# A decoder trunk on one core: x loaded by column halves around the first weight quantum, and the first norm's transposes in four PSUM banks

## The reference

```python
def _rmsnorm(x, g):
    y = x * rsqrt(mean(x * x, axis=-1) + 1e-6)
    return y * g
...
proj = _rmsnorm(h, norm_mix_even) @ w_in     # h = x at first; columns q, k, v, u, v' of 512 each
qa, ka, va, ub, vb = split(proj)
ws = where(causal, sgu_w, 0)                 # 4 x 128 x 128, used by the gated MLP
```

## Time and profile before

| | |
|---|---|
| time, median of 3 | 1388.93 us (1388.77 to 1390.04) |
| span of the profiled execution | 1387.2 us |
| time less span | 1.7 us |
| TensorE busy | 1364.8 us, 98% |
| VectorE, ScalarE busy | 82%, 73% |
| DMA, mean over the span | 315 GB/s |

### The profile page before, as it was taken

One profiled execution on the slowest core, in us unless ns is written; L12 is line 12 of the kernel. 1 busy time (PEld: TensorE's weight loads), 2 busy tenths in 40 slices (PEclk: granted clock), 3 DMA queues, 4 the chain that ended last, 5 costly groups with the idle time before them and its releaser, 6 DMA issues.

```text
span 1387.2 us, 19322 instructions
## 1 busy us (share of the span) xinstructions
PE 1364.8 (98%) x6874; PEld 1140.0 (82%) x6874; DVE 1133.7 (82%) x1154; ACT 1006.9 (73%) x1185; POOL 86.8 (6%) x117
## 2 busy tenths in 40 slices
PE   8999999999999999999999999999999999999997
PEld 7779989988788888888888888888888888888885
DVE  5675655556569999999999999899999989999996
ACT  5664544456548778778877877887787788788775
POOL 1201000000028500000000000000000000000010
PEclk9999999999999999999999999999999999999999
DMA  9457754353479999999999999999999999999960
GB/s 327 168 201 281 292 183 153 127 191 133 165 274 380 392 393 389 392 374 361 386 380 372 359 394 372 364 385 372 371 366 390 370 366 388 373 367 374 386 258 33
DMA packets 180621, 436.96 MB, mean 315 GB/s; under 512 B 4070, under 2 KB 8332, under 8 KB 180572
## 3 DMA queue, kind: packets, MB, share of 16 engines
q1 hardware_dynamic: 176816, 422.74, 82.8%
q0 software_dynamic: 3680, 13.54, 2.7%
q10 hardware_dynamic: 76, 0.02, 0.0%
HBM read 423.18 MB, written 13.11 MB: 315 GB/s over the span
## 4 chain that ended last, share of the span: by engine, by line
PE 93%; DVE 3%; ACT 3%; issue 1%; DMA 0%; ACTq 0%; DVEq 0%
PE ps L1607 26%; PE ps L1608 26%; PE ps L1609 26%; PE ps L1862 3%; PE ps L1864 3%; PE ps L1863 3%; PE ps L2134 2%; DVE w_lo L1054 1%; ACT w_hi L655 1%; DVE xt_lo L1093 0%; PE ps L1634 0%; PE ps L2102 0%; ACT e L710 0%; PE ps L1623 0%; PE ps L1617 0%
## 5 line engine op out<-in xcount | busy, mean ns | idle before, releaser
L1483 DVE TENSOR_TENSOR w_lo<-ring_a,w_hi 128x1024 fp32r<-128x1024 f32 x384 | 460.3, 1224 | 41.7 <-ACT w_hi L931 32.1
L931 ACT ACTIVATE w_hi<-ring_a 128x1024 fp32r<-128x1024 f32 x384 | 399.5, 1059 | 67.2 <-PE ps L1609 67.2
L1483 DVE TENSOR_TENSOR w_lo<-ring_b,w_hi 128x1024 fp32r<-128x1024 f32 x288 | 345.6, 1224 | 27.4 <-ACT w_hi L931 24.5
L1607 PE MATMUL ps<-w_hi,xg_hi 128*128 128x512 f32 x896 | 356.4, 398 | 0.0
L1608 PE MATMUL ps<-w_lo,xg_hi 128*128 128x512 f32 x896 | 353.0, 394 | 0.0
L1609 PE MATMUL ps<-w_hi,xg_lo 128*128 128x512 f32 x896 | 351.6, 392 | 0.0
L931 ACT ACTIVATE w_hi<-ring_b 128x1024 fp32r<-128x1024 f32 x288 | 300.8, 1058 | 55.3 <-PE ps L1609 55.3
L1054 DVE TENSOR_TENSOR w_lo<-ring_a,w_hi 128x1024 fp32r<-128x1024 f32 (+2 forms) x119 | 141.7, 1198 | 115.4 <-ACT w_hi L655 115.3
L655 ACT ACTIVATE w_hi<-ring_a 128x1024 fp32r<-128x1024 f32 (+2 forms) x119 | 121.9, 1033 | 129.7 <-PE ps L1864 65.2
L1607 PEld LDWEIGHTS ps<-w_hi,xg_hi 128*128 128x128 f32 x896 | 168.4, 188 | 38.6 <-DVE w_lo L1483 1.9
L1609 PEld LDWEIGHTS ps<-w_hi,xg_lo 128*128 128x128 f32 x896 | 168.3, 188 | 38.0
(11 more groups left out here) (333 smaller groups left out, 1387.0 us busy)
## 6 DMA issues: line engine op xcount, KB each, us to landing
ring_a<-in_moe_wg SPq DMA_DIRECT2D x40, 2048.0 KB, 9.8
ring_a<-in_moe_wu SPq DMA_DIRECT2D x32, 2048.0 KB, 9.9
ring_b<-in_moe_wd SPq DMA_DIRECT2D x32, 2048.0 KB, 9.7
ring_b<-in_moe_wu SPq DMA_DIRECT2D x24, 2048.0 KB, 10.3
ring_a<-in_moe_wd SPq DMA_DIRECT2D x24, 2048.0 KB, 9.5
ring_b<-in_moe_wg SPq DMA_DIRECT2D x16, 2048.0 KB, 10.4
ring_a<-in_ffn_wg SPq DMA_DIRECT2D x5, 2048.0 KB, 8.7
ring_a<-in_ffn_wu SPq DMA_DIRECT2D x5, 2048.0 KB, 7.8
```

The costliest lines, as they stand in the source:

```text
L931: nc.scalar.activation(w_hi[:, (Q1 + q) % NQ, 0:1024], slot(j % RING2)[:, 1024 * k:1024 * k + 1024], ACT.Copy).then_inc(hi_done, 1)
L1483: v.tensor_tensor(w_lo[:, (Q1 + q) % NQ, 0:1024], slot(j % RING2)[:, 1024 * k:1024 * k + 1024], w_hi[:, (Q1 + q) % NQ, 0:1024].bitcast(F32 ...
L1607: pe.matmul(out_, a_hi, w_hi[:, q, c0:c1], start=first, stop=False)
```

## The change

x is loaded in two pieces by column halves (both row tiles in each, rows of 2 KB in place of 4 KB), and q's first quantum is issued between them; the second half has a semaphore of its own, `x_rest`. The four groups of the first norm go into banks 6, 7, 2 and 3, so that no group waits for a bank; the fillers are now 6 ahead of x's first half and 6 between the halves (before: 8, 4 and 3), in bank 4. ScalarE's sums of squares wait for both halves.

```diff
         def fbank(k):
+            if k < 4:
+                return (6, 7, 2, 3)[k]
             return k % 2 if fills["mix_odd"] <= k < fills["mix_odd"] + 4 else 6 + k % 2
...
             sp.dma_start(table[:, 0:P], consts_d[:, 0:P]).then_inc(ident_in, 16)
-            for t in range(T):
-                sp.dma_start(h[:, t, :], A["x"][0].rearrange("(t p) d -> p t d", p=P)[:, t]).then_inc(x_in, 16)
+            x_rows = A["x"][0].rearrange("(t p) d -> p t d", p=P)
+            sp.dma_start(h[:, :, 0:512], x_rows[:, :, 0:512]).then_inc(x_in, 16)
             lead = units[0]
             per = lead.shape[0] // lead.quanta
             for k in range(lead.quanta):
+                if k == 1:
+                    sp.dma_start(h[:, :, 512:D], x_rows[:, :, 512:D]).then_inc(x_rest, 16)
                 sp.dma_start(slot(0)[:, k * lead.quantum:(k + 1) * lead.quantum].rearrange("p (c n) -> p c n", c=per),
...
-            act.wait_ge(x_in, 16 * T)
+            act.wait_ge(x_in, 16)
+            act.wait_ge(x_rest, 16)
...
             def bank_free(k):
-                if k >= 2:
+                if k >= 4:
                     pe.wait_ge(*emptied(k - 2))
...
-            keep_pace(8, 3, P)
-            pe.wait_ge(x_in, 16 * T)
-            for f in range(4):
+            keep_pace(6, 4, P)
+            pe.wait_ge(x_in, 16)
+            for f in range(2):
                 turn("mix_even", f, h_chunk)
-                if f == 1:
-                    keep_pace(4, 3, P)
-                elif f == 2:
-                    keep_pace(3, 3, P)
+            keep_pace(6, 4, P)
+            pe.wait_ge(x_rest, 16)
+            for f in range(2, 4):
+                turn("mix_even", f, h_chunk)
```

More of the change, by code:

```diff
@@ L307, in slot @@
             return ring_a[:, s] if s < RING1 else ring_b[:, s - RING1]
-        ident_in, const_in, x_in, lead_gain_in, grow_in, gain_in, even_in, bands_in, odd_in, rw_in = map(sem, (
-            "ident_in", "const_in", "x_in", "lead_gain_in", "grow_in", "gain_in", "even_in", "bands_in", "odd_in", "rw_in"))
+        ident_in, const_in, x_in, x_rest, lead_gain_in, grow_in, gain_in, even_in, bands_in, odd_in, rw_in = map(sem, (
+            "ident_in", "const_in", "x_in", "x_rest", "lead_gain_in", "grow_in", "gain_in", "even_in", "bands_in", "odd_in", "rw_in"))
         loaded = [sem(f"loaded{s}") for s in range(RING2)]
```

## The result

| | before | after |
|---|---|---|
| median (19 executions each) | 1389.08 us | 1391.61 us |
| lowest to highest | 1388.56 to 1390.55 | 1390.03 to 1392.95 |
| ratio | | 1.0016, 95% interval 1.0009 to 1.0023 |
| span of the profiled execution | 1387.2 us | 1390.9 us (its time 1392.65) |

The change makes the kernel slower by 2.5 us, 0.16 to 0.18%. That is inside the 0.2% that I called no change, but the interval excludes 1, and 1391.61 is 1.4 us above the top of my range. The profiled execution is the third slowest of the 19, so its span (+3.7) shows more than the median (+2.5).

A forecast was written before the change was run, and what follows sets the result against it. TensorE, busy 98% at full clock, was taken as the bound. A 2.25 us earlier start was lost to k's weights (1.1) and the mask (1.05), rounding to 0: 1388.9 us, range 1387.7 to 1390.2.

The forecast's parts named there:

- Step 1: Load queue at the start: x's halves land at 5.3 and 8.0 us, q's last quantum still at 12.0.
- two bounds: Effect of 2 KB rows at the queue's start: landings from 0.84 us earlier to 1.3 us later; 0 was taken.
- Step 2: Fillers ahead of x: with 6 calls the transposes start at 5.6 instead of 6.65, 1.05 us earlier.
- Step 3: Four banks: no bank wait for the second transposes; q projection starts at 9.9 instead of 12.16, 2.25 us earlier.
- Step 4: k's weights: w_lo is ready near 22.6 as before, so TensorE stands 1.1 us and keeps 1.15 us.
- Step 5: Masked sgu_w: the mask still ends at 26.4, TensorE stands 1.05 us, and none of the gain is kept.
- I find nothing later than 26.6 that differs: After sgu_w's transposes: the rest of the kernel keeps its times, leaving the span at 1387.2 us.
- The earlier mask: At sgu_w: the mask comes earlier, saving up to k's 1.15 us, 1387.8 us at best; chance 0.15.
- the fully kept 2.25 us: At the start: k's weights and the mask both over a microsecond earlier, time 1386.7 us; chance 0.03.
- The row limit: At the queue's start: x's first half lands up to 1.3 us later, time 1389.3 to 1390.2; chance 0.16.
- The falling clock: In TensorE's new pauses at 21.5 and 25.5 us: clock falls to 1.2 GHz, 1391.7 us or more; chance 0.03.

The follow-up runs named there:

- Experiment 1: The changed kernel with one wait less on ScalarE: only x_rest is waited for, issued behind the first half; 1389.11 us, ratio 0.9999.
- Experiment 5: The changed kernel with one wait less on ScalarE, and sgu_w's transposes behind k's second quantum instead of its first; 1388.61 us, ratio 0.9993.
- Experiment 8: The kernel before with the first norm's four groups in four banks and the fillers in bank 4, x still loaded by rows; 1389.12 us, ratio 0.9998.
- Experiment 2: The kernel before with nothing but one redundant wait on ScalarE, for a semaphore long set; 1392.32 us, ratio 1.0020.
- e7: The changed kernel with ScalarE's square root table load moved behind all but the last of the y_rows_out copies; 1390.00 us, ratio 1.0007.
- e6: The kernel before with two redundant waits on ScalarE, packed into one instruction (a shift of 1); 1392.49 us, ratio 1.0022.
- e10: The kernel before with 64 redundant waits on ScalarE, a shift of 32 instructions; 1391.43 us, ratio 1.0014.
- e9: The kernel before with 16 redundant waits on ScalarE, a shift of 8 instructions; 1391.91 us, ratio 1.0016.
- e5: The changed kernel with five filler products of 128x256 in TensorE's wait ahead of the last item's scatter; 1390.88 us, ratio 1.0014.

## Why the prediction was wrong, by its own steps

- **Step 1, x by halves: right but for 0.45 us.** q's last piece landed at 12.5 where I had 12.0, and k's at 20.9 where I had 20.3. The term is small beside what it varies by: GpSimd's first issue, which waits for q's last piece, stands between 12.23 and 13.39 us in the seven profiled executions with x's halves (mean 12.63), and between 11.98 and 12.74 in the seven with x by rows (mean 12.31). A loss of 0.3 us by the shorter rows is in line with that and not shown by it; my two bounds (-0.84, +1.3) hold it. That both kinds of rows are alike once under way I read from three of the page's four rows of such loads: the fourth, `ring_b<-in_moe_wg` with 2 KB rows, has 10.4 us.
- **Steps 2 and 3: right.** Transposes at 5.72 (5.6 forecast), the second set without a bank's wait, the first q product at 9.98 (9.9). The reason that I gave for the banks costing nothing was wrong in part: VectorE empties the fourth group only at 14.8, after q has begun. It costs nothing because q is written to banks 0 and 1, and k's products, which need banks 2 and 3, begin at 23.28.
- **Step 4, k's weights: right in kind.** TensorE stood 1.48 us (1.1 forecast), since the landing was 0.6 later; 0.53 us was kept in place of 1.15. Experiment 1, where k's `w_hi` began at 20.19, kept 1.25.
- **Step 5, the mask: right in kind, the number by luck.** The transposes of `sgu_w` start at 26.55, inside the forecast 26.5 to 26.7. The last landing was 0.5 earlier than I had, and the mask took 1.21 us instead of 0.68, which happened to make up for it. In experiment 1 the mask took 0.71 us, the transposes start at 25.97, and 0.65 us was kept where I had 0. Experiments 5 and 8 agree with the mask as the wait that decides.
- **The step that failed** is the sentence behind it, "I find nothing later than 26.6 that differs". The sum has no term for the added wait on ScalarE: I put it at nothing without giving a reason. For its own time that is right, for its place in the program it is not. Experiments 1 and 2 show that this one instruction is the whole loss of 2.5 us, some 1357 us later, at a loop that the change doesn't touch: there TensorE stands 2.41 us ahead of the scatter instead of 0.87. The pause of 0.91 us at that loop's exit was in the trace of before; I hadn't looked at the tail, since nothing of the change was there. None of the rivals had this either.
- **The rivals.** The earlier mask and the fully kept 2.25 us didn't come. The row limit could have given up to 1390.2, and the landings don't show it: x's first half landed at 4.9, ahead of the forecast 5.3. The falling clock's time, 1391.7, lies beside the measured 1391.61 by chance: most of the loss is the late scatter, the clock costs 1.6 us where it falls instead of 2.8, and it falls behind the tail's pause. At the place that I named it was seen in one profiled execution (`e7`), at a pause of 1.91 us; I had put a pause of 1.1 there, and the spread of k's landing, which I had no row for, makes it longer at times.

How the 2.5 us divide: the scatter's start is 1.44 us later, and with the clock kept in the tail the loss measures 1.75 (five fillers). The rest, 0.7 to 0.8 us, is a difference of medians whose intervals overlap, and it points to the clock. What the clock takes in an execution in which it falls can be read more sharply: from the start of the scatter to the end of TensorE's last product it is 6.05 or 6.06 us in all four traces in which it fell (after, `e2`, `e6`, `e10`) and 4.32 to 4.43 in the ten others, so 1.6 us. The mean clock recorded for each timed execution of the changed kernel fits this: the nine with 0.997 took 1391.44 to 1392.95 us, the five with 0.999 took 1390.04 to 1391.14. Where in these executions it fell is not recorded.

**What ScalarE stands for.** That it waits for its own program is inferred from four things: the pauses have no releaser, they sit at branches, they move with the number of instructions ahead, and the instruction queue is at work just then. The profile's view of the transfers from 1369 to 1373, in 40 slices of 0.1 us, holds nothing but three packets of 8 KB on one queue of kind "instruction"; each counts in the slice in which it starts. Before:

```profile
GB/s 0 0 0 0 0 0 0 0 0 0 0 0 0 0 0 82 0 0 0 0 0 0 0 0 82 0 0 0 0 0 0 0 0 0 0 0 82 0 0 0
...
q14 instruction: 3, 0.02, 2.0%
```

After:

```profile
GB/s 0 0 0 0 0 0 0 0 0 0 0 0 82 0 0 0 0 0 0 0 0 0 0 82 0 0 0 0 0 0 0 0 0 0 0 82 0 0 0 0
...
q14 instruction: 3, 0.02, 2.3%
```

By the packed traces the first packet comes from 1370.58 to 1370.89 before and from 1370.21 to 1370.76 after, and ScalarE goes on at 1372.02 and 1371.87, 1.13 and 1.11 us behind the packet's end. In all 14 traces this distance is 0.98 to 1.17 us. The second packet starts 0.93 to 1.19 us behind VectorE's branch in its own copy of the loop, so it is taken for VectorE's. Which packet belongs to which engine is not recorded.

This also says what the one instruction changes. From ScalarE's reaching the end of the loop's first turn (1369.69 before, 1369.59 after) until the missing code is there, 2.33 us pass before and 2.28 after: the code comes equally late in both kernels. Before, ScalarE has the loop itself at hand, runs its turns for 1.42 us meanwhile and stands only for the remaining 0.91 at the exit. After, it lacks the loop's last branch, stands for 2.24 us first and runs the other turns afterwards. With shifts of 8 and 32 it lacks the instruction ahead of that branch as well. So what is lost is not the length of the pause but the loop's turns that no longer run beside the loading, some 1.5 us.

The Trainium skill ("Runtime: NRT & Kernel Launch", Instruction fetch mechanics) says that instructions are loaded ahead in sequence only, and that a taken branch to a target that isn't loaded has to wait for it. The traces agree in kind: 2.04 to 2.41 us at a skipped body or ahead of it. By that rule alone the kernel before would be no exception, and it isn't: it has its 0.91 us at the exit.

## What to carry to other kernels

An edit that adds or takes one instruction on an engine moves all of that engine's later code; where this engine later branches on a value while another waits for it, list the pauses without a releaser around that branch before and after, since a wait "that costs nothing" can cost 2.5 us there. Test it with the unchanged kernel plus one idle wait before anything is said of the change itself. And an operation that nobody waits for, such as a table load, belongs behind the copy that is waited for: here that took away TensorE's wait ahead of the scatter. In the kernel before this gave 1.0 us in the medians, which the interval doesn't separate from nothing; together with the changed start, without the added instruction and with `sgu_w` later, it gave 1.4 us, which it does. The changed start alone gave nothing measurable.

## What I had not expected of the hardware

- A turn of the loop with its body skipped takes 0.65 to 0.75 us, and 2.04 to 2.41 us more in one place, by where the code lies; the same pause appeared with shifts of 1, 8 and 32 instructions.
- The clock falls in some executions of one program and not in others. Behind scatter waits of 2.03 us (`e10`), 2.25 (`e2`), 2.32 (`e6`) and 2.41 (after) it fell to 0.57 to 0.63 in the window from 1376 to 1380; in `e9`, with the same 2.03 us, it stayed at 1.00, and that execution took 1389.76 us where the median of `e9` is 1391.91. Behind waits of 0.36 to 1.17 us (`e5`, `e4`, `e12`, before, `e1`, `e7`) it stayed full.
- A mask of the same shape on GpSimd took 0.64 to 0.98 us in the other profiled executions and 1.21 after.
